# A two-block transformer step on one core: VectorE inverts 32x32 triangular blocks instead of 16x16, norms run in halves, and side work of TensorE is regrouped

## The reference, cut to what matters

```python
kk = jnp.einsum('bhncd,bhnsd->bhncs', k, k)
a_mat = jnp.where(tri_strict, beta[..., None] * kk * decay, 0.0)
...
sol = lax.linalg.triangular_solve(a_full, rhs, left_side=True, lower=True,
                                  unit_diagonal=True)
```

## Time and profile before

| | us |
|---|---|
| median of 3 runs | 885.01 (884.88 to 889.05) |
| the profiled execution, its own time | 886.16 |
| span of its trace | 884.4 |
| PE busy | 870.7 (98%) |
| DVE busy | 574.4 (65%) |
| ACT busy | 491.1 (56%) |
| POOL busy | 134.0 (15%) |

### The profile page before, as it was taken

The page is one execution under the profiler, slowest core; times in us unless marked ns, Lnnn a source line. Parts: engine busy times, 40 slices in busy tenths (PEclk is TensorE's granted clock), DMA queues, the critical chain, the costliest instruction groups (busy, mean ns, idle before and its releaser), DMA issues.

```text
span 884.4 us, 15704 instructions
## 1 busy us (share of the span) xinstructions
PE 870.7 (98%) x6514; PEld 807.0 (91%) x6514; DVE 574.4 (65%) x829; ACT 491.1 (56%) x745; POOL 134.0 (15%) x136
## 2 busy tenths in 40 slices
PE   8999999999999999999999999999999999999998
PEld 7999999889999988788899998999999899998886
DVE  5567664778888756666867887765477665554542
ACT  5556874566566645466675773434554575554330
POOL 5200001621111100123444110000200011120000
PEclk9999999999999999999999999999999999999999
DMA  7844374865655565347554444653246556666550
GB/s 275 279 152 134 98 238 147 273 224 161 203 197 184 184 221 193 139 156 275 172 159 146 144 144 143 174 179 96 96 145 222 175 174 193 191 193 228 176 186 25
DMA packets 132739, 156.87 MB, mean 177 GB/s; under 512 B 9369, under 2 KB 106044, under 8 KB 132412
## 3 DMA queue, kind: packets, MB, share of 16 engines
q1 hardware_dynamic: 125988, 152.30, 53.0%
q10 hardware_dynamic: 6680, 3.56, 1.3%
HBM read 153.61 MB, written 2.24 MB: 176 GB/s over the span
## 4 chain that ended last, share of the span: by engine, by line
PE 81%; DVE 9%; ACT 5%; issue 2%; POOL 2%; DMA 1%; SPq 0%; POOLq 0%; ACTq 0%
PE ps L2056 69%; PE ps L2087 3%; PE ps L2011 3%; DVE wl L835 2%; PE ps L2008 2%; ACT wh L1472 1%; PE ps L2110 1%; DVE gkq L869 1%; POOL wl L698 1%; DVE gv L869 1%; PE ps L2360 1%; DMA raw<-in_w_in 1%; PE ps L2330 1%; DVE mt L1293 1%; DVE sS L1091 0%
## 5 line engine op out<-in xcount | busy, mean ns | idle before, releaser
L835 DVE TENSOR_TENSOR wl<-raw,wh 128x1024 fp32r<-128x1024 f32 (+1 forms) x275 | 326.6, 1205 | 182.9 <-ACT wh L1472 182.8
L2056 PE MATMUL ps<-xh,wh 128*128 128x256 f32 x1248 | 348.4, 281 | 2.4 <-ACT xh L1520 2.0
L1472 ACT ACTIVATE wh<-raw 128x1024 fp32r<-128x1024 f32 (+1 forms) x292 | 286.9, 1023 | 111.6 <-PE ps L2056 89.6
L2056 PE MATMUL ps<-xh,wl 128*128 128x256 f32 x1248 | 342.8, 277 | 0.0
L2056 PE MATMUL ps<-xl,wh 128*128 128x256 f32 x1248 | 341.6, 277 | 0.0
L2056 PEld LDWEIGHTS ps<-xh,wh 128*128 128x128 f32 x1248 | 233.5, 188 | 4.5 <-ACT wh L1472 1.7
L2056 PEld LDWEIGHTS ps<-xh,wl 128*128 128x128 f32 x1248 | 233.4, 188 | 0.0
L2056 PEld LDWEIGHTS ps<-xl,wh 128*128 128x128 f32 x1248 | 232.9, 188 | 0.3
L698 POOL TENSOR_TENSOR wl<-raw,wh 128x1024 fp32r<-128x1024 f32 (+1 forms) x17 | 44.3, 2603 | 162.0 <-ACT wh L1472 161.8
L2056 PE MATMUL ps<-wh,f2L 128*128 128x512 f32 x128 | 49.8, 389 | 0.0
L2056 PE MATMUL ps<-wh,f2H 128*128 128x512 f32 x128 | 49.8, 389 | 0.0
(11 more groups left out here) (357 smaller groups left out, 1360.7 us busy)
## 6 DMA issues: line engine op xcount, KB each, us to landing
raw<-in_w_in SPq DMA_DIRECT2D x55, 1024.0 KB, 5.1
raw<-in_w_up SPq DMA_DIRECT2D x38, 1024.0 KB, 5.2
raw<-in_w_down SPq DMA_DIRECT2D x26, 1024.0 KB, 5.0
raw<-in_w_out SPq DMA_DIRECT2D x8, 1024.0 KB, 5.1
raw<-in_w_proj_fox SPq DMA_DIRECT2D x4, 1024.0 KB, 5.1
raw<-in_w_proj_gdn SPq DMA_DIRECT2D x4, 1024.0 KB, 5.0
raw<-in_w_conv_branch SPq DMA_DIRECT2D x4, 512.0 KB, 3.4
raw<-in_w_att_branch SPq DMA_DIRECT2D x4, 512.0 KB, 3.4
```

The lines of the kernel that those rows point to most:

```text
L835: e.tensor_tensor(L, R, H.bitcast(F32), ALU.subtract).then_inc(lo.sem)
L1472: e.activation(tile_of(WH, u)[:, k:kc, :], tile_of(RAW, u)[:, k:kc, :], ACT.Copy).then_inc(hi.sem)
L2056: k = e.matmul(o, l, r, start=opens, stop=done and n == ends[c], skip_group_check=True)
```

## The change

- **Inversion:** 32x32 blocks. U32 holds each of the 64 blocks on two partitions (the same data twice), and each partition has every second row of the inverse, 16 rows of 32. DVE does 31 steps of two instructions instead of 15, on up to 136 elements instead of 64, from tick 49, one step about every 0.8 tick. The write of the inverses and the read of the blocks are two transfers each.
- **Doubling:** `LEVELS` is (32, 64): two levels at ticks 95 and 104 instead of three at 75, 84 and 93. `SOLVE` is 113 for both groups at once, with steps 4 ticks apart; `o_turn` moves to unit 104, tick 5 (143).
- **Key products:** two heads to a stretch, at 21, 24, 27, 30, and no `settle(5)`. The v transposes all come at tick 54.
- **Norms:** DVE adds to XRES in two halves, and ACT squares each half as it comes; POOL sums the halves. The `low` halves of units 30 to 32 that POOL did go to DVE, and the order of `low` and `high` at the two boundaries changes. The load of unit 33 is issued ahead of a load of gains.
- **Forgetting attention:** the next head's scores follow the product with v at once, and `o_low`, `o_high` move into the next head's turn: 19 ticks per pair of heads instead of 22.

```diff
-POOL_HALF = frozenset([0, *range(26, 33), *range(78, 87)])
-LEVELS = (16, 32, 64)
-LAST = 2
+POOL_HALF = frozenset([0, *range(26, 30), *range(78, 87)])
+LEVELS = (32, 64)
+LAST = 1
...
 def squares_at(r):
-    return (9, 11, 14, 18)[r // 2]
+    return (9, 9, 14, 18)[r // 2]
...
 def head_at(h):
-    return 21 + h + h // 2
-
-
-BLOCKS_OUT, BLOCKS_IN, INVERT, INVERSES_OUT, INVERSES_IN, START_Y = 33, 40, 47, 55, 59, 65
+    return 21 + 3 * (h // 2)
+
+
+BLOCKS_OUT, BLOCKS_IN, INVERT, INVERSES_OUT, INVERSES_IN, START_Y = 33, 40, 49, 76, 80, 88
...
 def turn_v_at(c):
-    return 54 + 4 * (c // 2)
+    return 54
...
 def level_at(c, i):
-    return 75 + 9 * i
-
-
-def solve_at(g):
-    return 106 + 2 * g
+    return 95 + 9 * i
+
+
+SOLVE = 113
...
-                mac(XRES[:, a, :], FG[:, a, :], rs[:, 2 + a:3 + a], XRES[:, a, :]).then_inc(px.sem)
+                for k in (0, 512):
+                    mac(XRES[:, a, k:k + 512], FG[:, a, k:k + 512], rs[:, 2 + a:3 + a], XRES[:, a, k:k + 512]).then_inc(px.sem)
...
-                for m in range(15):
-                    n, k = m + 1, 15 - m
-                    t = T16[:, 0:n * k].rearrange("p (i j) -> p i j", i=n)
-                    v = Y16[:, 0:n, n:16]
+                for m in range(31):
+                    c, n, k = m + 1, m // 2 + 1, 31 - m
+                    t = T32[:, 0:n * k].rearrange("p (r j) -> p r j", r=n)
+                    v = Y32[:, 0:n, c:32]
...
-                    if m % 2:
-                        yield from at.to(INVERT + (m + 1) // 2)
+                    yield from at.to(INVERT + 4 * c // 5)
...
+            def squares_of_halves(n, a):
+                for h, k in enumerate((0, 512)):
+                    e.wait_ge(*px(("lo", "x")[h], 2 * n - 2 + a))
+                    e.activation(FG[:, a, k:k + 512], XRES[:, a, k:k + 512], ACT.Square, scale=D ** -0.5,
+                                 accum_out=gv_[:, 11, a, 2 + h:3 + h]).then_inc(nsh.sem)
...
-                e.dma_start(U16[:], blocks[:].rearrange("a s t -> (a s t)").rearrange("(p x) -> p x", p=P)[:, 0:16 * P].rearrange(
-                    "p (i t) -> p i t", t=P)[:, :, 0:16]).then_inc(blocks_in, 16)
+                for rows in (LO_, UP_):
+                    e.dma_start(U32[rows], diagonal).then_inc(blocks_in, 16)
                 yield from at.to(INVERSES_OUT)
-                e.wait_ge(*b16("s", 14))
-                e.dma_start(inverses[:], Y16[:].rearrange("p i j -> p (i j)")).then_inc(inverses_out, 16)
+                e.wait_ge(*b16("s", 30))
+                flat_ = inverses[:].rearrange("p x -> (p x)")
+                by_parity = flat_.rearrange("(g r z j) -> z g r j", g=64, r=16, z=2)
+                for z, rows in enumerate((LO_, UP_)):
+                    e.dma_start(by_parity[z], Y32[rows]).then_inc(inverses_out, 16)
                 yield from at.to(INVERSES_IN)
-                e.wait_ge(inverses_out, 16)
+                e.wait_ge(inverses_out, 32)
...
                     mul(O[:, 128:256], fvm[:, 1, h * P:(h + 1) * P], sT[s][:, 256:384], False, True).then_inc(me.sem)
-                    yield from pause(3)
+                    if i < 3:
+                        scores(i + 1)
```

More of the change, by code:

```diff
@@ L304, in two_blocks @@
                     "ul0", "ul", "ob0", "ob", "mk0", "mk1", "mk", "ml0",
-                    *(f"ml{i}{k}" for i in range(2) for k in "abc"), "mlh", "m0", "m1", "m2", "pp")
+                    *(f"ml{i}{k}" for i in range(LAST) for k in "abc"), "mlh", "m0", "m1", "m2", "pp")
         nsq = steps("norm_sq", "sq")
         nrs = steps("norm_rstd", "var", "pow")
+        nsh = steps("norm_sq_half", "lo", "up")
         nsc = steps("norm_scaled", "lo", "up")
@@ L364, in two_blocks @@
         fox_act = [steps(f"fox_act{i}", "x0", "x1", "n0", "n1", "sT", "oh") for i in range(2)]
-        fox_dve = [steps(f"fox_dve{i}", "b0", "b1", "mask", "r0", "r1", "rec", "ol") for i in range(2)]
+        fox_dve = [steps(f"fox_dve{i}", "b0", "b1", "mask", "r0", "r1", "rec") for i in range(2)]
+        fox_low = [steps(f"fox_low{i}", "ol") for i in range(2)]
         sums_out, sums_in, gates_in = (sem(n) for n in ("sums_out", "sums_in", "gates_in"))
@@ L579, in sync @@
             e.dma_start(GP[:], norm_mix_post[0].partition_broadcast(P)).then_inc(ld_gp, 16)
-            for u in range(NRAW, U_UP + 1):
+            for u in range(NRAW, U_UP + 2):
                 weights(u)
@@ L583, in sync @@
             e.dma_start(GN[:], norm_ffn_pre[0].partition_broadcast(P)).then_inc(ld_gn, 16)
-            for u in range(U_UP + 1, U_UP + 5):
+            for u in range(U_UP + 2, U_UP + 5):
                 weights(u)
@@ L1133, in gdn @@
                 e.wait_ge(*epl("E", 3))
[L1134 to L1140, removed]
@@ L1347, in vector @@
             low(U_FQ + 1, 0)
+            low(U_FQ + 1, 1)
             x2_low(2, 0, 0)
+            post(1, U_FQ - 1, 1, 1, ends=False)
             x2_low(2, 0, 1)
-            post(1, U_FQ - 1, 1, 1)
-            low(U_FQ + 1, 1)
+            post_ends(1, 1)
             low(U_FQ + 2, 0)
+            low(U_FQ + 2, 1)
             x2_scaled(2, 1)
-            low(U_FQ + 2, 1)
             x2_low(2, 1, 0)
@@ L1397, in vector @@
             for i in range(4):
-                unit(U_G2 + i, 5 if i == 1 else None, lambda: side.add(o_turn()))
+                unit(U_G2 + i, 5 if i == 2 else None, lambda: side.add(o_turn()))
             for i in range(4):
@@ L2280, in fox_attention, with scores @@
                 S, O, sc = PS[3 + s], PS[5 + s], sS[s]
-                me, ac, dv = fox_pe[s], fox_act[s], fox_dve[s]
-                yield from pause(15)
-                for i in range(4):
+                me, ac = fox_pe[s], fox_act[s]
+                def scores(i):
                     h = s + 2 * i
-                    e.wait_ge(*fnk("fin", 7))
                     if i:
                         e.wait_ge(*ac("sT", i - 1))
-                    else:
-                        e.wait_ge(*sdv("GG"))
                     mul(S[:, 0:128], fqT[:, h, 0:128], fkT[:, h, 0, :])
@@ L2293, in fox_attention @@
                         settle(7)
+                yield from pause(15)
+                e.wait_ge(*fnk("fin", 7))
+                e.wait_ge(*sdv("GG"))
+                scores(0)
+                for i in range(4):
+                    h = s + 2 * i
                     yield from pause(15)
@@ L2499, in tensor @@
                 unit(U_GB + 2 * i, XH, XL)
-                unit(U_GB + 2 * i + 1, obH, obL, lambda q: fox_act[q % 2]("oh", q // 2), lambda q: fox_dve[q % 2]("ol", q // 2))
+                unit(U_GB + 2 * i + 1, obH, obL, lambda q: fox_act[q % 2]("oh", q // 2), lambda q: fox_low[q % 2]("ol", q // 2))
             for u in range(U_GZ, U_YG):
-                unit(u, XH, XL, at=5 if u == U_G2 + 1 else None, begins=lambda: side.add(o_turn()))
+                unit(u, XH, XL, at=5 if u == U_G2 + 2 else None, begins=lambda: side.add(o_turn()))
             for i in range(4):
```

209 lines of the change are left out of this document (114 added, 95 removed).

## The result

The changed kernel takes 890.17 us (median of 8 runs, 887.51 to 890.59), the kernel before on the same chip 885.13 us; the ratio is 1.0037 with a 95% interval of 1.0022 to 1.0052. I had forecast 885.0, no change. The interval leaves out 1, so the kernel is slower, a little but clearly: by 3.3 us in the ratio and by 4.2 us between the two profiled executions (span 888.6 against 884.4).

A forecast was written before the change was run, and what follows sets the result against it. PE was taken to bound the kernel, busy 870.7 of 884.4 us. Gains of 6.2, 2.2, 0.8 and 1.0 against costs of 9.7 and 0.5 summed to 0.0: 885.0 us, own range 880.3 to 889.3, 8 in 10 876 to 890.5.

The forecast's parts named there:

- Norms: At the first and second norm, halved squares and reordered `low` work shorten PE's waits: a gain of 2.2 us.
- key products: At the key products, two heads to a stretch need one wait for DVE per pair: a gain of 0.8 us.
- the level: The doubling level of 16x16 blocks goes, with its 16 transposes and two stretches of 64 instructions: a gain of 6.2 us.
- PE's arrival at tick 95: At the first remaining doubling level, PE was to arrive at 589.7 us on the profile's clock.
- The inversion's wait: Ahead of the first remaining level, PE waits for the longer chain of DVE steps and transfers: a cost of 9.7 us.
- the line: In the inversion, a step of two DVE instructions was to cost 0.39 us plus 0.0021 per element.
- DVE's sum: From the inversion's first step to its last, DVE needs 28.0 us: 18.1 for steps, 9.9 for work between them.
- Rival A: The inversion stays hidden and only the gains are left: 875.3 us with no wait; chance 0.30.
- rival B: The inversion's transfers cost by bytes, U taking 8.8 us or more and Yc 11: 893.9 us; chance 0.15.
- Merged stretches and attention: In the attention and transposing stretches, fewer stretches and shorter waits: a gain of 1.0 us, bounds -1 and 1.5.
- The tail: Behind the solves, unit 106 needs the last oaL up to 0.7 us before it is ready: a cost of 0.5 us.

The follow-up runs named there:

- e2_norms_keys: The kernel before with only the halved norms and the key products in pairs: 882.57 us, ratio 0.9965 to the kernel before.
- half-steps run: The changed kernel with 16 of the 31 inversion steps, so its result is not the reference's: 883.81 us, ratio 0.9927 to the kernel before.
- the second trace: The changed kernel run once more, unaltered, on another chip: 893.45 us, ratio 1.0039 to the kernel before.
- e11_v_on_act: The changed kernel with the four scalings of turned v on ScalarE instead of VectorE: 891.38 us, ratio 1.0020 to the kernel before.
- e6_pool_lows: The changed kernel with the second `low` halves of units 93 to 98 on GpSimd instead of VectorE: 897.93 us, ratio 1.0090 to the kernel before.
- e12_late_levels: The changed kernel with both levels, the solves and `o_turn` 6 ticks later: 895.05 us, ratio 1.0053 to the kernel before.

## Why the prediction was wrong

**Norms, key products, the level, PE's arrival at tick 95:** right. -0.9 and -1.5 us for -0.9 and -1.3; -1.1 for -0.8 (1.8 in e2_norms_keys); 145 records fewer; PE at tick 95 at 589.65 for 589.7.

**The inversion's wait:** right in size, 8.9 us for 9.7 (a third of it as `wl` waits, as said), and its links erred in both directions: the steps took 26.7 us for 28.0, since a step was 0.54 us on average where the line gave 0.58; from the write's issue to the read's 5.9 for 4.1; read 5.6 for 5.2; from the issue of U's read to the first step 7.3 for 7.2. The last agreement is luck. I had charged 2.7 us for 2048 more runs, and the parts of U landed after 4.8 and 5.8 us, 0.4 to 1.4 more than before; the rest of the 7.3 is DVE's `low` behind ACT's long issue, which I had not in the chain. The write was too low for another reason than I had weighed, by all signs the weight load beside it. The half-steps run confirms that most of the wait is DVE's sum. Rival A (0.30) would have needed DVE some 9 us sooner, and rival B (0.15) 8.8 us for U and 11 for Yc, where they took 5.3 and 5.6.

**The step that failed first is one that isn't in the sum:** what a wait of 6 us does to PE's clock. The transposes behind it and the work after them ran at the lower level, 1.9 us here, 3.0 in the second trace (14.28 and 15.38 for 12.35), next to nothing in the run that kept PE busy (12.61). I had costed PE's idle time and taken the work behind it at its old rows.

**Merged stretches and attention, -1.0:** wrong in sign, +0.3. The waits for `sS` went as I assumed and one for `sT` took their place (+0.7), inside my bound of 1 us; what was not in it is the slower pace of the matmuls. Over the attention's main work they stand 116.3 ns apart on average for 113.7 before, which for the 522 matmuls of this stretch is 1.4 us by my estimate, the whole miss.

**The tail, +0.5:** the wait itself is right, 0.3 us by the waits and 0.6 by the starts of the matmuls. The other 1.8 us of that row is the pace in that execution, and the second trace had only 0.4 of it. By these two traces it belongs to the spread between executions more than to the change.

**Together:** -6.2 and the gains of 3.5 us (norms and keys) stand against 8.9 of waits, 1.9 of clock, 0.6 of tail and the attention's 0.3, which makes +2.0 us. The inversion's row of the table has 1.0 us more (5.6 for -6.2 + 8.9 + 1.9 = 4.6), of which I can place about half, as slower pace at best; the rest stays open. That gives 3.0, near the ratio's 3.3 us; the span's 4.2 has the tail's 1.8 us of pace in it and the start's -0.6. With the clock's 1.9 us in the sum and the attention at 0 it would have been +2.9, still within 0.5% but on the right side.

## What to carry over

A wait of PE costs more than its length: count what runs behind it at the lower clock, and look where a wait goes when it is moved along a chain with little slack. Before work moves from the engine that bounds to one that is idle a third of the time, add up the chain that has to end by a tick, with everything that stands between its links in the engine's order; the helper's average load says nothing. Count as well what runs beside a transfer: here the write of the inverses took 1.7 us ahead of a weight load and 5.0 just behind one. Of a bundle of edits each should be run alone: here the two small ones, norms and key products, are worth 2.8 us without the large one, which costs 5.8.

## What I had not expected of the hardware

**Two paces of PE at the same clock.** 256-column matmuls without a gap follow each other at 113.3 or at 117.8 ns, with the granted clock at 1.00 both times, for 50 to 170 us on end; where I looked, the pace changed only where side work or a wait came between. It differs between executions of the same code (210 to 270 us, 668 to 693 us), and behind the last norm (700 us on) six of the eight traces from the two slower chips had 117.8 and all others 113.3. In the attention it goes with the code: the nine traces with the new rhythm have means of 116.2 to 117.2 ns, the five with the old one 113.7 to 113.9. What picks the pace stays open; no run varied it alone.

**The clock does not go by the wait's length alone.** It fell in waits of 5.3 to 6.9 us (e11_v_on_act, the changed kernel, e6_pool_lows), stayed up at 2.6 (e6_pool_lows, a second wait) and fell behind one of 1.8 (e12_late_levels).

**A small DVE instruction can take 2 us** where GpSimd's `low` runs at the same time, ten times its own length (1.84 and 2.28 us for 0.18); the kernel before has GpSimd's `low` only where DVE has no chain of small steps.
